# In-projection of an encoder: token tiles normalised before they are transposed, and the first two weight blocks multiplied group by group while the tokens arrive

## The reference, cut to what matters

```python
def rmsnorm(x, g, eps=EPS):
    xf = x.astype(jnp.float32)
    xf = xf * lax.rsqrt(jnp.mean(xf * xf, axis=-1, keepdims=True) + eps)
    return (xf * g.astype(jnp.float32)).astype(x.dtype)

h = rmsnorm(x, attn_norm[j])          # x: 2304 tokens x 1024
proj = h @ w_in                       # w_in: 1024 x 4096
q, k, v, z = jnp.split(proj, 4, axis=-1)
...                                   # attention with ALiBi, per head
o = o.reshape(B, S, D) * jax.nn.silu(z)
```

## Time and profile before

| | |
|---|---|
| median of three timed runs | 3275.3 us (3273.77 to 3275.41) |
| the profiled execution | 3275.25 us |
| its span in the trace | 3273.6 us |
| PE busy | 2995.3 us, 91% of the span |
| token phase (start to first unit of PE) | 0 to 72.6 us |
| units of the in-projection | 72.6 to 862.1 us |
| first DMA issue of the attention stage | 865.9 us |

### The profile page before, as it was taken

One profiled execution on the slowest core, in us unless ns is written; L12 is line 12 of the kernel. 1 busy time (PEld: TensorE's weight loads), 2 busy tenths in 40 slices (PEclk: granted clock), 3 DMA queues, 4 the chain that ended last, 5 costly groups with the idle time before them and its releaser, 6 DMA issues. The chain is left out here.

```text
span 3273.6 us, 42276 instructions
## 1 busy us (share of the span) xinstructions
PE 2995.3 (91%) x15084; PEld 2511.9 (77%) x15084; DVE 1605.8 (49%) x1832; ACT 1341.3 (41%) x2294; POOL 788.7 (24%) x392
## 2 busy tenths in 40 slices
PE   6999999999689999999999999995998898996599
PEld 4888888888568787878787878783677898975487
DVE  7323221111178787878787878784774101431222
ACT  6111100011167776667676767673342322221221
POOL 1223223223022222212121212123331320220552
PEclk9999999999899999999999999997999998898799
DMA  5333332222434313131313131104453513444653
GB/s 171 119 114 113 125 103 67 75 66 67 111 95 151 99 33 99 34 99 33 97 34 93 40 91 41 38 28 160 165 189 114 194 68 105 119 134 144 238 178 109
DMA packets 226332, 340.27 MB, mean 104 GB/s; under 512 B 22315, under 2 KB 172139, under 8 KB 220668
## 3 DMA queue, kind: packets, MB, share of 16 engines
q1 hardware_dynamic: 221548, 321.23, 31.1%
q0 software_dynamic: 4608, 16.78, 1.9%
HBM read 224.68 MB, written 126.03 MB: 107 GB/s over the span
## 5 line engine op out<-in xcount | busy, mean ns | idle before, releaser
L817 DVE TENSOR_REDUCE pa_half_max<-pa_score 128x1 f32<-128x1024 f32 x512 | 625.4, 1222 | 287.7 <-PE pa_score L630 287.7
L760 ACT ACTIVATE pa_p<-pa_score,pa_neg_max 128x1024 f32<-128x1024 f32 x512 | 567.2, 1111 | 74.4 <-DVE pa_neg_max L823 71.1
L894 POOL TENSOR_SCALAR pa_p<-pa_p,pa_inv_sum,pa_lam_neg 128x2048 f32<-128x2048 f32 x128 | 262.6, 2052 | 1072.9 <-DVE pa_inv_sum L844 1072.9
L687 PE MATMUL pa_o_acc<-pa_wt,pa_vv 128*128 128x256 f32 x2048 | 506.6, 381 | 0.1
L626 PE MATMUL pa_score<-pa_ka,pa_qa 128*128 128x512 f32 x1024 | 462.4, 452 | 39.9 <-DMA pa_kb<-const_position 27.0
L118 PE MATMUL ia_acc<-ia_xh,ia_wh 128*128 128x512 f32 (+1 forms) x1280 | 471.8, 369 | 0.0
L119 PE MATMUL ia_acc<-ia_xl,ia_wh 128*128 128x512 f32 (+1 forms) x1280 | 471.7, 368 | 0.0
L120 PE MATMUL ia_acc<-ia_xh,ia_wl 128*128 128x512 f32 (+1 forms) x1280 | 471.4, 368 | 0.0
L630 PE MATMUL pa_score<-pa_kb,pa_qb 96*128 96x512 f32 x1024 | 433.6, 423 | 0.0
L740 ACT ACTIVATE pa_wt<-pa_turned 128x512 f32<-128x512 f32 x512 | 306.0, 598 | 298.6 <-PE pa_turned L658 298.2
L687 PEld LDWEIGHTS pa_o_acc<-pa_wt,pa_vv 128*128 128x128 f32 x2048 | 371.4, 191 | 43.6 <-issue 0.3
(11 more groups left out here) (224 smaller groups left out, 4355.3 us busy)
## 6 DMA issues: line engine op xcount, KB each, us to landing
ia_raw<-attn_w_in POOLq DMA_DIRECT2D x32, 512.0 KB, 5.5
qk_hi<-ia_stage SPq DMA_DIRECT2D x64, 256.0 KB, 2.1
qk_lo<-ia_stage SPq DMA_DIRECT2D x64, 256.0 KB, 2.1
pa_ka<-qk_hi SPq DMA_DIRECT2D x32, 512.0 KB, 6.6
fl_slices<-normed SPq DMA_DIRECT2D x26, 512.0 KB, 6.6
pa_vt<-v SPq DMA_DIRECT2D x8, 1152.0 KB, 5.5
oa_b_in<-o SPq DMA_DIRECT2D x18, 512.0 KB, 4.8
oa_g_in<-attn_gate SPq DMA_DIRECT2D x18, 512.0 KB, 5.9
```

The costliest lines, as they stand in the source:

```text
L687: mm = pe.matmul(o_acc[:], vv[:, k], wt[:, g % 2, k], start=k == 0, stop=k == NB - 1)
L760: act.activation(dst[:, half * HALF:(half + 1) * HALF], score[:, (4 * q + j) % RING].rearrange("p a b -> p (a b)"), ACT.Exp, bias=neg_max[ ...
L817: dve.tensor_reduce(half_max[:, q % 2, n, half:half + 1], score[:, (4 * q + j) % RING].rearrange("p a b -> p (a b)"), AX_X, ALU.max).then_ ...
L894: pool.tensor_scalar(p1[:, par], p1[:, par], inv_sum[:, par, 1:2], lam["neg"][:, 0:1], ALU.mult, ALU.mult).then_inc(p1_scaled, 1)
```

## The change

Each tile of tokens is now finished by itself, before and behind its transpose:

- SP loads rows into three slots (L211). ACT squares them along the row with an accumulated sum (L334) and takes the root of that one column (L336); DVE takes the reciprocal (L366); POOL multiplies the rows by it in place (L253).
- PE transposes the normalised rows (L294). DVE multiplies by the norm's weight, which now lies along the partitions, from PSUM into a new buffer `h` of two slots (L374). ACT copies `h` to `xh` (L341); the low part `h - xh` is DVE's (L379) for even tiles and for the tiles up to 6, POOL's (L257) for the odd tiles from 7 on.
- The matmuls with ones, the wide roots and reciprocals, and the multiplication of each unit by 1/rms (L350) are gone. A unit is taken from PSUM by ACT (L355) and, for split blocks, its low part by DVE (L396).
- Weights need no norm: POOL copies `raw` to `wh` (L244) and subtracts (L248), from two slots of `raw`.
- The first ten units are written out: after six transposed tiles, blocks 0 and 1 are multiplied in group 0, then in groups 1 and 2, then block 0 and block 1 in groups 3 and 4 each. Two more tiles are transposed ahead of each of the units 1 to 6. Those units use banks 4 to 7, the transposes banks 0 to 3. The other 30 blocks run as before.

```diff
+    ROWS = 3
+    EARLY = 6
...
+        def lo_of_pool(t):
+            return t % 2 == 1 and t > EARLY
...
+        first_units = [(g, u) for g in range(NG - 2) for u in range(2)] + [(g, u) for u in range(2) for g in (NG - 2, NG - 1)]
...
+                def scale(t):
+                    s = t % ROWS
+                    pool.wait_ge(inverted, t + 1)
+                    pool.tensor_scalar(xr[:, s], xr[:, s], rstd[:, s:s + 1], None, ALU.mult).then_inc(scaled, 1)
...
+                def turn(t):
+                    pe.wait_ge(scaled, t + 1)
+                    wait(pe, normed, t - 1)
+                    for k in range(KB):
+                        mm = pe.transpose(x_tile(t)[:, k], xr[:, t % ROWS, k * P:(k + 1) * P], ident[:])
+                    mm.then_inc(turned, 1)
...
-                    pe.wait_ge(scaled, unit + 1)
...
+                for n, blk, u, g, s, kind, dest, w_no, _ in units(pe):
+                    if isinstance(n, int) and n < BEGUN:
+                        upto = min(EARLY + 2 * n, NT)
+                        for t in range(ready, upto):
+                            turn(t)
+                        ready = upto
+                        pe.wait_ge(w_lo, u + 1)
+                        last = sum(GROUPS[g]) // P
+                        wait(pe, x_lo, lows(last, False))
+                        wait(pe, x_lo_pool, lows(last, True))
+                        wait(pe, out_lo, n - 3)
+                    else:
...
+                            if u == 0 and g == 0:
+
+                                pe.wait_ge(out_lo, N_SPLIT)
...
+                def square(t):
+                    s = t % ROWS
+                    act.wait_ge(x_in[s], 16 * (t // ROWS + 1))
+                    act.activation(squares[:], xr[:, s], ACT.Square, accum_out=square_sum[:, s:s + 1]).then_inc(row_sums, 1)
+                    act.wait_ge(row_sums, t + 1)
+                    act.activation(root[:, s:s + 1], square_sum[:, s:s + 1], ACT.Sqrt, bias=eps[:, 0:1],
+                                   scale=1.0 / D).then_inc(rooted, 1)
...
+                        for t in range(0 if n == 0 else EARLY + 2 * n, min(EARLY + 2 * n + 2, NT + 2)):
+                            if t >= 2:
+                                token_high(t - 2)
+                            if t < NT:
+                                square(t)
...
+                            if t < NT:
+                                inverse(t)
+                            if t >= 2 and not lo_of_pool(t - 2):
+                                token_low(t - 2)
+                            if 1 <= t <= NT:
+                                scale_columns(t - 1)
...
-                    dve.tensor_tensor(stage[:, s, :n], acc[:, g, :n], rstd[:, t0:t0 + n],
-                                      ALU.mult).then_inc(scaled, 1)
```

More of the change, by code:

```diff
@@ L200, in units, with x_tile, bank @@
                 blocks0 += blocks
-                his += NG * blocks if kind != "plain" else 0
-                los += NG * blocks if kind == "split" else 0
                 stores += per * NG * blocks // 2
             units.stores = stores
+        def x_tile(t):
+            return acc[:, 2 * (t % 2):2 * (t % 2) + 2, :].rearrange("p a (b t) -> p (a b) t", t=P)
+        def bank(n, g):
+            return 4 + n % 4 if isinstance(n, int) and n < BEGUN else g
         with nc.Block() as block:
@@ L208, in _ @@
             def _(sp):
[L209 to L223, removed]
-                    t0, n = GROUPS[g]
[L225 to L231, removed]
+                loaded = 0
@@ new lines, in _ @@
+                for u in range(2):
+                    load(u, u)
+                for t in range(NT):
+                    scale(t)
+                    if 2 <= t < 6:
+                        (high, low)[t % 2](t // 2 - 1, t // 2 - 1)
+                    if t >= 2 and lo_of_pool(t - 2):
+                        token_low(t - 2)
+                token_low(NT - 1)
+                for u in range(2):
+                    pool.wait_ge(w_lo, u + 1)
+                    load(2 + u, u)
+                for u in range(2):
+                    pool.wait_ge(products, ends[u])
+                    high(2 + u, u)
+                    low(2 + u, u)
@@ L263, in _ @@
+                with pool.Fori(0, all_blocks // 2 - 2) as j:
+                    for u in range(2):
+                        b = 2 * j + 4 + u
+                        pool.wait_ge(w_lo, b - 1)
+                        load(b, u)
+                        hold(pool, pool_held, products, NG * (b - 1))
+                        high(b, u)
+                        low(b, u)
             @block.tensor
             def _(pe):
-                pe.sem_inc(products, NG)
-                pe.sem_inc(transposed, 2)
@@ L279, in _ @@
[L279 to L290, removed]
-                    pe.wait_ge(scaled, unit + 1)
-                    three_pass(pe, acc[:, g, :n], lambda k: wh[:, u, k], lambda k: wl[:, u, k],
-                               lambda k: xh[:, k, t0:t0 + n], lambda k: xl[:, k, t0:t0 + n],
-                               range(KB)).then_inc(products, 1)
+                pe.wait_ge(consts_in, 32)
@@ L297, in _ @@
             @block.scalar
             def _(act):
[L299 to L306, removed]
-                        act.activation(square(s).rearrange("p (k t) -> p k t", k=KB), x_tile(s),
-                                       ACT.Square).then_inc(squared, 1)
@@ L309, in _ @@
[L309 to L322 removed]
+                act.wait_ge(consts_set, 1)
@@ new lines, in _ @@
+                for n, blk, u, g, s, kind, dest, _, slot_stores in units(act):
+                    if isinstance(n, int) and n < BEGUN:
+                        for t in range(0 if n == 0 else EARLY + 2 * n, min(EARLY + 2 * n + 2, NT + 2)):
[3 more added lines that the diff above has]
+                                square(t)
+                    width = GROUPS[g][1]
+                    act.wait_ge(products, n + 1)
+                    wait(act, stored[s], slot_stores)
+                    out = stage[:, s, :width]
+                    act.activation(out.bitcast(F32R) if kind == "split" else out, acc[:, bank(n, g), :width],
+                                   ACT.Silu if kind == "silu" else ACT.Copy).then_inc(out_hi, 1)
```

212 lines of the change are left out of this document (106 added, 106 removed).

## The result

| | before | changed |
|---|---|---|
| median of 20 timed runs each | 3274.23 us (3270.48 to 3278.45) | 3281.32 us (3273.64 to 3285.02) |
| ratio | 1 | 1.0020, 95% interval 1.0013 to 1.0027 |
| the profiled execution (span) | 3275.25 us (3273.6) | 3279.66 us (3277.7) |
| first matmul of unit 0 | 72.6 us | 39.05 us |
| first matmul of block 2 | 122.1 us | 129.1 us |

The account below looks back on a forecast made before the run. PE alone bounds the units, DVE's low part the token phase. Block 2 earlier -6.6, boundary +1.3, tail -0.4, clock +1.5 made -4.2; with half of 1.0, -3.9: 3271.3 us, range 3265.5 to 3279.

Parts of the forecast that it names:

- row scaling on POOL 1.20: POOL's multiplication of a token tile by 1/rms takes 1.20 us, with ends of 1.05 and 1.98.
- the waits: PE's standing still between units 0 and 9, for scaled tiles and low parts: 5.4 us in all.
- The clock: PE's granted clock falls to 1.2 GHz after turn 1, before unit 0: +1.5 us, ends 0 and 4.5.
- the ring: Token loop over DVE and ACT, high part of t-1 before square of t+1: 5.1 us per tile.
- The turns, 12 x 1.97 = 23.6: PE's transposes of the 12 tiles between units 0 and 9, 1.97 us each: 23.6 us.
- rival 1: PE's clock stays up and POOL is at its cheap end: -5.7 to -7.0 us, down to 3268.2; chance 0.30.
- The boundary: First plain unit waits for the last split unit's low part, a gap of PE: +1.3 us once, ends 0.9 and 1.8.
- The tail: Last unit leaves through ACT alone instead of DVE and ACT: -0.4 us.
- Rival 3: Crowded queue or late block 2 weights delay PE; at 4 us lost nothing is won, 3275; chance 0.13.
- The block of 24.67 us: Each weight block after the token phase still takes PE 24.67 us, as before.
- half of 1.0: Allowance for a slow first turn of PE, 1.0 us, thought less likely than not.
- Rival 2: POOL's row scaling wins the shared port before DVE's low part, 6.1 us per step: 3280 or more; chance 0.12.

Follow-up runs that it names:

- a1: Changed kernel with POOL's row scaling written with two operations (times 1/rms, times 1.0) instead of one: 3268.52 us, 0.9983 of the kernel before.
- c1: Changed kernel with PE's token-phase waits filled by transposes of the identity, whose results are overwritten: 3274.08 us, 1.0001 of the kernel before.
- The two edits together: Changed kernel with two-operation row scaling and, on ACT, the square of tile t ahead of the high part of t-2: 3246.26 us, 0.9925 of before.

## Why the prediction was wrong, point by point

- **The step that failed: "row scaling on POOL 1.20", with ends 1.05 and 1.98.** It measured 2.84 us. I had drawn the line through two rows of a TENSOR_SCALAR that does two operations, and took the form with one to cost the same or less. a1 shows that the operation count is what differs: the same data, one more multiplication, 1.11 us. My upper end was the price of an instruction with two tensor inputs, again on the ground that less work cannot be dearer. a1 puts the step at 16.3 us of block 2's start, more than the whole miss of 13.8 (129.1 against 115.3). With the price that I had assumed the kernel comes out 5.4 to 5.7 us faster than before, where I had forecast 4.
- **Where the 13.8 us lie.** Unit 0 started at 39.05 instead of 37.0 (2.05), the four slow units cost 10.3, turns and waits together 1.45. The dear scaling lengthens the waits, and the clock falls in them: filling them alone gives back 9.6 (c1).
- **The clock, priced once at 1.5 us, measured 9.6 (c1).** I had the mechanism and the direction, but applied it to the ring in front of unit 0 alone. With waits of 2.9 us and then 0.6 to 1.3 before units 2, 4 and 6 it came back three times. The two terms are one: with the scaling at 1.11 us the same four units lose about 4 us (6.16, 5.53, 7.12, 7.01 against 5.48 in a1's trace), not 10.3.
- **The turns, 12 x 1.97 = 23.6, were mis-sized and hidden.** 1.97 us a tile is the time at 1.2 GHz; between the units a tile takes 1.09, and two take 1.7 from start to next start, so 12 are about 10. PE's own share is 13 us less than I said, and the waits are that much longer: 20 instead of 5.4, counted from start to start (16.0 in PE's idle records). The sum of turns and waits, 29 forecast, about 30 found, was right by luck: the chain over ACT, DVE and POOL sets the pace and PE's part is in its shadow.

**The clock at the start.** I wrote that the trace disagrees with the Trainium skill's rule since the first transposes ran at 1.00. The column was wrong, not the rule. Eight transposes took 1.97 us throughout the first 39 us and 1.09 later, and in the window 39 to 43 us the granted clock reads 1.00 while the matmuls of unit 0 are 0.43 us apart:

```profile
39.00:43.00 4.00, 4.00 (x11) 3.17 (x10) 2.93 (x2) 1.04 (x2) 4.00 (x2) 1.00 0.40 131
```

0.43 us for 512 columns is the spacing at which the column reads 0.50 (62 to 66 us), and 0.23 the one at which it reads 1.00 (68 to 70), so unit 0 started at 1.2 GHz. Its matmuls go from 0.43 to 0.23 us apart at 43.5 us, and the column does not show it: it reads 1.00 from the start to 60 us. Before its first recorded change it says nothing here. The old token phase, whose transposes took the same 1.97 us, ran at 1.2 GHz too; so rival 1's ground, a clock of 1.00 in that phase, was not there. The Trainium skill (TensorE: Matmul & The Clock Gate, Part 1), by which the throttled clock is the default, agrees with these durations.

- **What held.** The ring: 5.1 us forecast, 4.91 found (22.35 to 27.26, DVE's reciprocals), and 6.12 where POOL overran. The first rows at 4.33 us instead of 5.5. The boundary: 1.3 forecast, 1.28 found. The tail: -0.4, found -0.46. Rival 3 did not come: PE waited for no weights before block 2, and ACT only once, 2.3 us, for rows behind the first. POOL waits for DVE at the port where DVE starts first, as in most steps (8 of DVE's 12 low parts took 1.2 us). The block of 24.67 us.
- **Two slips in the sum.** -4.2 and half of 1.0 make -3.7, not -3.9, so the sum gives 3271.6. Block 2 of the kernel before started at 122.13 in the trace, not at the reckoned 121.9. Neither matters to the outcome.
- **Rival 2** came nearest in outcome (slower), and part of its mechanism was there: 4 of 12 low parts took 2.42 to 2.44 us, 1.2 of it behind POOL, not because POOL won the start but because its previous instruction had not ended. I had put the point from which the kernel is slower by 0.2% at 1.4 us of scaling with POOL first; it was found at 2.84 with DVE mostly first.
- The chance of 0.12 for slower was too small, since it hung on a price that I had held below 1.98 by an argument and not by a row.

## What to carry to other kernels

Price an instruction by a row of the same form, down to its number of operations; where the trace has none, the range must reach well above the nearest row, because a simpler form can be dearer. When a chain goes round several engines, write it as a ring and see which instruction in it needs no result of the others: putting the square ahead of the high part was worth 20 us at no cost. A wait of PE costs more than its length if the clock falls in it; check by durations. If the wait can't be removed, matmuls without use, into a bank that will be overwritten, can hold the clock, as in c1. The two edits together turn this change from 0.2% slower to 0.75% faster than before (0.9925), and that version beats both kernels.

## What the runs showed of the hardware that I had not expected

- POOL's TENSOR_SCALAR on 128x1024 float32, in place: 2.84 us with one multiplication, 1.11 with two; the one-operation form takes 0.75 on DVE. POOL's CAST of the same size takes 1.03. Why the one-operation form is slow stays open.
- The granted clock reads 1.00 up to its first recorded change (60 us in the changed kernel), with matmuls 0.43 and 0.23 us apart alike.
- Eight float32 transposes of 128x128 take 1.97 us at 1.2 GHz and 1.09 at 2.4 GHz.
- PE's clock fell in waits of 2.9 and 1.3 us with one tile of 1.09 between them, and the unit after them took 8.12 us instead of 5.48; with the waits filled down to 0.4 us it did not fall. In c1 units 4 and 6 too took 5.55 us, with up to 1.3 us of waiting left in one stretch.
